# Norms of a two-layer float32 trunk on one core: the order of the square root and the weight split, an earlier table load, and products on constants in three norms

## What is computed

```python
def rms_norm(x, g=None, eps=NORM_EPS):
    xf = x.astype(F32)
    y = xf * lax.rsqrt(jnp.mean(xf * xf, axis=-1, keepdims=True) + eps)
    ...
def modulate(h, shift, scale):
    return h * (1.0 + scale) + shift
...
    for i in range(DEPTH):
        ...
        hl = modulate(rms_norm(xl, norm1_g[i]), sh1, sc1)
        hc = modulate(rms_norm(xc, norm1_g[i]), csh1, csc1)
        ...
        xl = xl + g1 * ol
        xl = xl + g2 * conv_ffn(modulate(rms_norm(xl, norm2_g[i]), sh2, sc2), ...)
        if need_ctx:
            xc = xc + cg1 * oc
            xc = xc + cg2 * conv_ffn(modulate(rms_norm(xc, norm2_g[i]), csh2, csc2), ...)
    return rms_norm(xl, final_norm_g)
```

## Time and profile before

| | |
|---|---|
| median of 3 runs | 2069.78 us (2066.95 to 2076.1) |
| profiled execution | 2067.73 us, of which the span of the trace is 2065.9 us |
| granted clock of TensorE, mean of the span | 0.966 of full speed |
| norm A: last product before it to first product after it | 687.5 to 700.5 us |
| norm B | 1295.6 to 1312.3 us |
| norm C | 1669.9 to 1681.1 us |
| norm D: last product of the block to the end | 2051.2 to 2065.9 us |

### The profile page before, as it was taken

How to read it: one execution, slowest core, us unless ns; L and a number is a source line. 1 busy time by engine, 2 the same in 40 slices (tenths; PEclk the granted TensorE clock), 3 DMA queues, 4 the chain that set the end, 5 groups by cost and what they waited for, 6 DMA issues and landing times.

```text
span 2065.9 us, 25915 instructions
## 1 busy us (share of the span) xinstructions
PE 1947.7 (94%) x10776; PEld 1632.0 (79%) x10776; DVE 1189.8 (58%) x2032; ACT 692.0 (33%) x1049; POOL 22.4 (1%) x18
## 2 busy tenths in 40 slices
PE   4999999999888899999999999799899889999997
PEld 2999999999877788888888888665565568888885
DVE  3465556555763675426652555655265469578485
ACT  3333333333322333213321333345245344233242
POOL 0000000000210000000000000000000000000000
PEclk8999999999999899999999999889889999999998
DMA  6221222112201133323322332110000123333333
GB/s 272 92 91 37 78 82 82 62 56 78 82 1 51 51 113 123 101 87 119 122 88 97 123 103 75 62 31 1 31 31 1 41 72 95 99 92 92 102 93 101
DMA packets 45332, 165.82 MB, mean 80 GB/s; under 512 B 4896, under 2 KB 5280, under 8 KB 45088
## 3 DMA queue, kind: packets, MB, share of 16 engines
q1 hardware_dynamic: 45216, 164.16, 23.9%
HBM read 162.05 MB, written 2.10 MB: 79 GB/s over the span
## 4 chain that ended last, share of the span: by engine, by line
PE 89%; DVE 6%; DMA 2%; ACT 2%; issue 1%; SPq 0%; DVEq 0%
PE slot L389 27%; PE slot L378 8%; PE slot L379 8%; PE slot L380 8%; PE MA L529 4%; PE slot L779 4%; PE slot L781 4%; PE slot L780 4%; PE slot L714 4%; PE MB L447 2%; PE MA L779 2%; PE MA L780 2%; PE MA L781 2%; PE slot L705 2%; DMA AD<-in_ada 1%; PE MB L480 1%
## 5 line engine op out<-in xcount | busy, mean ns | idle before, releaser
L1167 DVE TENSOR_TENSOR WL<-WR,WH 128x1024 fp32r<-128x1024 f32 x204 | 249.3, 1223 | 235.5 <-ACT WH L834 234.4
L834 ACT ACTIVATE WH<-WR 128x1024 fp32r<-128x1024 f32 x204 | 215.3, 1056 | 409.7 <-DMA WR<-in_w 409.7
L378 PE MATMUL slot<-HH,WH 128*128 128x384 f32 (+2 forms) x896 | 324.8, 363 | 27.8 <-DVE HL L1265 14.7
L379 PE MATMUL slot<-HL,WH 128*128 128x384 f32 (+2 forms) x896 | 311.8, 348 | 0.0
L380 PE MATMUL slot<-HH,WL 128*128 128x384 f32 (+2 forms) x896 | 311.5, 348 | 0.0
L378 PEld LDWEIGHTS slot<-HH,WH 128*128 128x128 f32 x896 | 172.0, 192 | 55.8 <-issue 35.0
L389 PE MATMUL slot<-HH,WH 128*128 128x256 f32 (+1 forms) x768 | 198.7, 340 | 2.5 <-DVE ACC L1490 1.6
L389 PE MATMUL slot<-HL,WH 128*128 128x256 f32 (+1 forms) x768 | 195.9, 337 | 0.0
L389 PE MATMUL slot<-HH,WL 128*128 128x256 f32 (+1 forms) x768 | 195.7, 337 | 0.0
L379 PEld LDWEIGHTS slot<-HL,WH 128*128 128x128 f32 x896 | 172.2, 192 | 9.5 <-issue 2.2
L380 PEld LDWEIGHTS slot<-HH,WL 128*128 128x128 f32 x896 | 171.4, 191 | 8.8
(11 more groups left out here) (228 smaller groups left out, 3116.0 us busy)
## 6 DMA issues: line engine op xcount, KB each, us to landing
WR<-in_w SPq DMA_DIRECT2D x204, 512.0 KB, 3.6
ada_raw<-in_ada SPq DMA_DIRECT2D x84, 512.0 KB, 4.6
AD<-in_ada SPq DMA_DIRECT2D x3, 2048.0 KB, 23.5
X<-in_x SPq DMA_DIRECT2D x1, 3072.0 KB, 12.5
out<-Y SPq DMA_DIRECT2D x8, 256.0 KB, 2.2
Y<-in_masks SPq DMA_DIRECT2D x1, 512.0 KB, 19.8
ada_raw<-in_rope SPq DMA_DIRECT2D x1, 512.0 KB, 3.4
small<-in_small SPq DMA_DIRECT2D x1, 327.5 KB, 3.1
```

Of the source, the lines that this page charges most:

```text
L378: mm(SLOT[s][:, po], WH[w % NB][:, k, :], hi[:, k, to], start=(k == 0), stop=False)
L379: mm(SLOT[s][:, po], WH[w % NB][:, k, :], lo[:, k, to], start=False, stop=False)
L834: go(WH[t % NB][:, :, :], WR[t % NB][:, :, :], ACT.Copy).then_inc(w_hi_done, 1)
L1167: tt(WL[t % NB][:, :, :], WR[t % NB][:, :, :], WH[t % NB][:, :, :].bitcast(F32), ALU.subtract).then_inc(w_split, 1)
```

## The change

Five edits, all at the norms:

- `norm_act` (ScalarE) takes the square root without splitting a tile ahead of it. The third tile is split after the second chunk's HH instead.
- A square root of the constant `eps_t` into a new column `sqrt_set` stands between the first and the second square, so that the table of the square root is loaded there.
- `norm_dve` (VectorE) leaves out the split ahead of `coef` and makes it behind the sixth chunk's HL.
- SP issues the rope tables behind tile T_AT + 2 instead of T_AT + 1.
- `norm_pe` (TensorE) gets products of the identity with 256 columns of `small`, written to an unused part of MA: six ahead of the wait for the squares, one between the sums and the spread, seven behind the spread. This is done in the norms A, B and C; norm D is called with `more=False`.

```diff
--- before.py
+++ after.py
@@ -118,6 +118,7 @@
         ident = sb("ident", [P, P])
         ones = sb("ones", [P, 1])
         eps_t = sb("eps_t", [P, 1])
+        sqrt_set = sb("sqrt_set", [P, 1])
         masks = sb("masks", [P, LEVELS + 1, P], U8)
         small = sb("small", [P, NSMALL])
         sig_c = sb("sig_c", [P, KC, 2])
@@ -329,7 +330,7 @@
                 for _ in range(PIECES.get(t, 0)):
                     load_piece(n)
                     n += 1
-                if t == T_AT + 1:
+                if t == T_AT + 2:
                     for s in range(2):
                         sp.wait_ge(evacuated[s], T_AT // 2)
                     sp.dma_start(rope[:, :, :], rope_in).then_inc(rope_done, 16)
@@ -480,12 +481,23 @@
                     last = mm(MB[:, chunk(c)], rstd6[:, c:c + 1].to_broadcast([P, P]), ident[:, :], start=True, stop=True)
                 last.then_inc(rstd_spread, 1)
 
-            def norm_pe(first):
+            def keep_busy(n):
+
+                for _ in range(n):
+                    mm(MA[:, 512:768], ident[:, :], small[:, 0:256], start=True, stop=True)
+
+            def norm_pe(first, more=True):
                 sums.add(KC - 1)
+                if more:
+                    keep_busy(6)
                 pe.wait_ge(sq_added, sums.now())
                 pe.wait_ge(ada_ready, rows.now())
                 token_sums(SSQ, first)
+                if more:
+                    keep_busy(1)
                 spread(first)
+                if more:
+                    keep_busy(7)
 
             pe.wait_ge(silu_ready, 1)
             for g in range(ADA_FIRST):
@@ -815,7 +827,7 @@
                             lat_products(opened, k, n, GH, GL)
 
             lat_feed_forward()
-            norm_pe(CCH)
+            norm_pe(CCH, more=False)
 
 
         @block.scalar
@@ -863,6 +875,8 @@
             def norm_act(tokens, shift, tiles=None, early=False, ring=None):
                 t = slice(TOK - tokens, TOK)
                 for c in range(KC if tiles is not None else 0):
+                    if c == 1:
+                        go(sqrt_set[:, :], eps_t[:, :], ACT.Sqrt)
                     if tiles is not None:
                         split_high(tiles + c + AHEAD)
                         if ring is None:
@@ -870,13 +884,16 @@
                         else:
                             act.wait_ge(slot_free[(ring + c) % NS], (ring + c) // NS + 1)
                     square(c, t)
-                split_high(tile.now() + AHEAD)
                 if not early:
                     added.add(KC - 1)
                     token_std(1.0 / D, (TOK - tokens) // P)
                 if shift is None:
                     return
+                if early:
+                    split_high(tile.now() + AHEAD)
                 for c in range(KC):
+                    if c == 2:
+                        split_high(tile.now() + AHEAD)
                     norms.add()
                     act.wait_ge(normed, norms.now())
                     for _, to, v in spans(tokens):
@@ -1238,8 +1255,6 @@
                 squares.add(KC)
                 if scale is not None:
                     dve.wait_ge(ada_ready, rows.now())
-                    if not early:
-                        split_low(tile.now() + AHEAD)
                     link(stt(coef[:, :, :], ada[:, scale:scale + KC, :], 1.0, gain.unsqueeze(2).to_broadcast([P, KC, 2]), ALU.add, ALU.mult))
                 if not early:
                     token_rstd((TOK - tokens) // P)
@@ -1271,6 +1286,8 @@
                     if c + 1 < KC:
                         scaled(c + 1)
                     low(c)
+                    if c == 5 and not early:
+                        split_low(tile.now() + AHEAD)
 
             def mixer_lo(tokens, first=0):
                 t = slice(TOK - tokens, TOK)
```

## The result

| | before | changed |
|---|---|---|
| median | 2069.78 us (9 runs) | 2056.07 us (9 runs, 2052.75 to 2064.9) |
| ratio, with its 95% interval | | 0.9944 (0.9927 to 0.996), that is 11.6 us less (8.3 to 15.1); the two medians stand 13.7 us apart, and gains below go by such ratios |
| profiled execution | 2067.73, span 2065.9 | 2064.9, span 2063.1: the slowest of its nine |
| granted clock, mean of the span | 0.966 | 0.971 |

What follows compares the result with a forecast made beforehand. TensorE, busy 94%, was taken to bound the kernel, with idle time and half clock at the norms. Gains of 2.8 (A), 5.0 (B) and 3.4 (C) sum to 11.2 us off the median 2069.78: 2058.6, range 2054.5 to 2065.

Steps and rivals of the forecast that it cites:

- Spread starts: Norms A, B, C: root directly after sums puts the spread at 692.8, 1300.9, 1674.25 (before: 693.91, 1305.72, 1676.57).
- Sums and products on constants: Ahead of the spread: sums take 1.5, 1.5, 1.05 us; six constant products, 0.43 each, fit in TensorE's idle time at no cost.
- rival 3: Ahead of the sums: 256-column products cost 0.86 each, or the six run at half clock; slower, 2076 us; chance 0.05.
- Does the clock hold?: Norms A, B, C: constant products keep the clock up through the spread; called the weak step, gain 11.2 or else 8.3 us.
- rival 1: Norms A and B: clock falls ahead of the spread, 2.93 instead of 1.50; gain 8.3, time 2061.5; chance 0.28.
- Rival 2: Norms A, B, C: constant products do not act on the clock, spreads stay slow; no change, 2069.7 us; chance 0.07.
- The sum: From the norms to the end of the next block's first two tiles: gains A 2.8, B 5.0, C 3.4, sum 11.2 us.
- The moved split: VectorE's split after the sixth chunk delays chunks 6 and 7, on the path: 1.2 us in A and B.
- Zero for early table and rope tables: At the norms: early table load and small root, and rope tables after the third tile's weights, each costed at zero.
- The seven products: Behind the spread: 3.0 us against 3.66 idle in A, costing nothing; in rival 1 they bring the clock back.
- Nothing between the norms: Stretches between norms: only TensorE's own work counts there, at full clock; the sum has no term for them.
- rival 4: Behind the norms: following tiles' weights arrive too late and the gain is given back, some 5 us at most; 2064; chance 0.07.

Runs made afterwards that it cites:

- the products alone: Kernel before plus only the fourteen products on constants in norms A, B and C: 2064.03 us, ratio 0.9987.
- column of 64 bytes: Changed kernel with its new column widened from 4 to 64 bytes per partition: one profile, A 29.0, B 28.3, C 20.1 us; no total time given.
- the repetition: Changed kernel unaltered, run once more beside three others on one chip: 2055.7 us, ratio 0.9953.
- the order: Changed kernel without any product on constants: 2057.51 us, ratio 0.9957.
- column only: Kernel before with one unused 4-byte column allocated, no instruction changed: 2070.33 us, ratio 1.0013.
- split later: Changed kernel with VectorE's split of the third tile behind the last chunk instead of the sixth: 2058.21 us, ratio 0.9952.

## Why the prediction was right, and where it was not

The time came out in the range, and the chain of the norms is as foreseen. The clock, the column and the total are not.

- **Spread starts.** Foreseen at 5.35, 5.33 and 4.33 us after the last product (692.8, 1300.9, 1674.25 less 687.45, 1295.57, 1669.92); measured 5.31, 5.32 and 4.30.
- **Sums and products on constants.** 1.50, 1.50 and 1.05 as foreseen. Six of the constant products took 2.75 with the tail of the last; from one to the next it is 0.43, as foreseen, so rival 3 (0.86) is out. They fit: 2.75 of the 3.16 us that TensorE idled in A and B. In C, where it idled 2.62, they fill the wait to its end, and the sums start 2.61 us after the last product, so they were not late there either.
- **Does the clock hold?** The forecast said yes in all three and called this the weak step. In neither profile of the change did it hold in all three. Over the ten profiles the spread kept it in C always, in A in 5 and in B in 3. So rival 1's fall at the spread is real, in more than half the cases, and the step "I forecast that the clock holds" was wrong as a rule. Its price was 1.45 us a norm foreseen, 1.3 measured. Rival 2 is out: with the products alone A's spread took 1.61 instead of 2.93.
- **The sum.** Where the clock held in all three, with the column of 64 bytes: A 31.9 - 29.0 = 2.9 (foreseen 2.8), B 33.4 - 28.3 = 5.1 (5.0), C 3.6 (3.4), in all 11.6 against 11.2. In the profiled execution of the change: 1.6, 3.8 and 3.6, 9.0, against rival 1's 8.3.
- **The moved split** is on the path, as foreseen, but at 1.0 us a norm and not 1.2. The experiment that moved it behind the last HL got it back.
- **Zero for early table and rope tables.** Right for the norms, by one profile each. The argument for the table was weaker than it could be: I costed what the early load might do, and did not see that, once the split is gone, the load hides under the wait for the sums anyway. Two of the five edits do nothing for the norms, and one of these two brought the column.
- **The seven products.** Foreseen as harmless, and in rival 1 as what brings the clock back. It comes back without them; they prevent a second fall, for which nothing waits. The prediction checked that they fit in A alone (3.66 us); in C, with 2.47, they do not quite, and the first product starts 0.2 us later.
- **Nothing between the norms.** Wrong. The diff's first line, `sqrt_set = sb(...)`, stands in no term of the sum. It cost 4.7 us in the feed-forward, net about 3.5. So rival 4, a gain given back in the stretches behind the norms, was right in its outcome there and wrong in its mechanism: no weights arrive late, and the products themselves stand further apart.
- **The total.** By the terms that the traces carry, 9.0 to 11.6 less 3.5 is 5.5 to 8.1 us. The measured difference is 11.6 (8.3 to 15.1), and 9.7 (6.0 to 13.2) in the repetition. What fills the gap is not settled. So it was in part luck that 2058.6 came out close: the column left out and the unexplained rest of the gap went against each other.
- **What may fill the gap.** That the median's distance to the profiled execution was lower clock in these norms, which I gave 0.11, cannot be tested by it: the time at half clock outside the norms moves by more than that from one execution to the next (before norm A 34 us in the one trace of before and 31 to 51 in the others; from B's first tiles to C 51, and 31 to 55 in the others). The profiled execution of the change had 51 before norm A, and its norm A began 5.8 us later than before. Over all executions the mean granted clock is 0.967 for the kernel before (57 of them), 0.977 for the change (15), 0.974 for the order and 0.973 for the products alone. Some 2 x 0.010 x 2060 = 41 us less at half clock go with the change, where the norms in the two traces account for 34 (41.0 before, 6.8 after). So part of the gap may be half clock elsewhere. What such time goes with, the traces show between B and C: 332.2 us with 31 of them at half clock (column only), 341.7 with 55 (split later), some 0.4 us for each. For the 7 us left over that makes an estimate of 3 us, about the size of the gap. That is argued, not shown: nothing says that the change is what lessens half clock outside the norms.

## What to carry to other kernels

Between the last partial sum and what hangs on it, nothing should stand in a queue that waits for a transfer; once that is mended, small edits around it (an early table load, an earlier transfer) may already be worth nothing. Products on constants paid here where the wait they fill was the last thing that pulled the clock down: ahead of the sums, and not behind the spread, where another engine set the pace. And a declaration is an edit: compare the durations of untouched products before and after, since here tensors that moved cost as much as a norm gave.

## What the runs showed of the hardware

- Four bytes allocated and never used changed the mean length of TensorE's 512-column products in the down tiles of layer 0's feed-forward from 392 to 397 ns, and the start-to-start distance to the product behind from 0.2295 to 0.2347 us. Elsewhere it went down (384-column products before norm A: 0.1777 to 0.1773).
- At full clock a float32 product of 128 x 256 follows the one before it after 0.43 us; a run of six takes 2.75 with the tail of the last.
- Identical code at an identical place met a full clock in one execution and half in another: 12 records in 1.60 or 2.93 us.
- The granted clock followed what TensorE had done before, not what it was doing. Without the seven it was at 1.00 from 700.8 to 704.2, where TensorE worked for 0.32 us, and at 0.50 from 704.2 to 707.6, where it worked throughout.
